# Moving the down projection of a two-layer network's FFN ahead of the up projection of the same step

## The chip, the cores and the metric

The kernel runs on one core of a Trainium2 chip. The metric is device time in microseconds (us) for one execution of the whole program. A core has five engines that run their own instruction streams and wait for each other by semaphores: TensorE (PE, matrix products; its weight loads are listed apart as PEld), VectorE (DVE), ScalarE (ACT), GpSimd (POOL) and SyncE (SP), which here issues the weight transfers.

## The reference

Two blocks of two layers each work on 256 tokens of width 1024. The second block's layers end in a convolutional FFN, which is the part that matters here (D_FF is 3072, the convolution spans 3 tokens):

```python
def conv_ffn(x, norm, w_up, dw_w, dw_b, w_down):
    h = rms_norm_2(x, norm) @ w_up
    g = causal_dwconv(h[..., :D_FF], dw_w, dw_b)
    u = h[..., D_FF:]
    return (jax.nn.gelu(g) * u) @ w_down

def second_block(...):
    for layer in range(DEPTH):
        ...                                   # mixer_ab or conformer_conv
        x = x + cross_attn(...)
        x = x + conv_ffn(...)
    return rms_norm_2(x, final_norm)
```

## The kernel before

**Stages.** The program runs through stages L0, L1 (first block), AB, X0, F0, C, X1, F1 (second block) and the final norm. F0 and F1 are the two FFNs. Each engine has its own function with the same stages written out in order, so the order of the source is the order of each engine's queue.

**Weights.** All weights go through one stream of units of 128 x 1024 numbers, listed in order by `weight_order()`. SP loads unit n into one of 5 raw buffers (`RAW`) once the unit 5 in front has been split. A unit is then split for an exact product: ACT copies it to `weights_hi` (line 485), DVE subtracts that to get `weights_lo` (line 915). There are 4 buffers of split units (`SPLIT`), and ACT may write one only when PE is done with the unit 4 in front. The function `splitter` decides where ACT and DVE stand in their queues with this: before an engine waits for a tile of PE (`for_tile`), it emits the splits of all units which that tile needs and of up to three units behind them. Where one engine waits for a mark of the other (`after_vec`, `after_act`), it emits the splits that the other had emitted by then.

**Products.** Each product is three passes: hi x hi, lo x hi, hi x lo. `proj_F` (line 1467) makes 512 output features x 256 tokens with the weights standing in PE: 4 units of 24 products of 256 columns. `proj_T` (line 1449) makes tokens x 512 features with the activations standing: its products have 512 columns, 12 to a unit.

**The FFN** takes the 3072 inner features in six chunks j of 512. For chunk j there are a gate projection g j, an up projection u j (both `proj_F`, 4 units each) and a down projection d j (`down`, two `proj_T` of 2 units each), which adds into banks 4 to 7 over all chunks. Between them on ACT and DVE:

- after g j: ACT scales four tiles (line 851), DVE adds the other two taps of the convolution (line 1323, 8 instructions), ACT applies the gelu (line 854);
- after u j: DVE multiplies u by the gelu's result (line 1328, two instructions, one for each bank), ACT copies the product to the high part (line 841), DVE makes the low part (line 1331), which is marked `h{j}lo`.

`down(j)` waits for `h{j}lo` ahead of its first product, since both parts are read from the start:

```python
                def down(j):
                    for n in range(2):
                        proj_T("o", 2 * n, src=F_HL[j % 2], us=(0, 1), first=j == 0, last=j == 5, ready=f"h{j}lo")
```

g and u use banks 0 to 3 in turn. Behind d 5 the residual is added (line 999). In stage C, which comes after F0, PE starts with a projection of the memory (4 units, `k`) that needs none of it, then transposes the normed tokens (line 1489). After F1 come only the last norm (line 1390) and the store.

Of the kernel before, what the change touches and what calls it, by code (L numbers as in the profile page):

```python
# [16 lines left out]
W = D // 2  # L17
# [92 lines left out]
def build(nc, A, out, known):  # L110
# [5 lines left out]
    with ctx:  # L116
# [124 lines left out]
        def bank(C, name, i=0):  # L241
            return ps[PLACE[C.stage, name, i]]

        def halves(b):
            return b[:, :].rearrange("p (j s) -> p j s", j=2)
# [5 lines left out]
        def weight_order():  # L251

            got = []

            def kmaj(name, lead):
                ap = A[name]
                for i in lead:
                    ap = ap[i]
                return ap.rearrange("(k p) n -> p k n", p=P)

            def col(name, lead, c, us=(0, 1, 2, 3)):
                ap = kmaj(name, lead)
                got.extend((True, ap[:, 2 * u:2 * u + 2, c:c + W]) for u in us)

            def crossed(name, lead):
                for us in ((0, 1), (2, 3)):
                    for n in range(2):
                        col(name, lead, n * W, us)

            def plain(ap):  # L270
                got.append((False, ap))

            def win(l, *at):
                for c in at:
                    col("w_in", (l,), c)

            def chunk(name, lead, j):
                for n in range(2):
                    col(name, lead, n * W, (2 * j, 2 * j + 1))

            for l in range(DEPTH):
                mem_k, mem_v = (lambda: col("w_mem_kv", (l,), 0)), (lambda: col("w_mem_kv", (l,), W))
                if l:
                    mem_k()
                win(l, SBQ, SBK)
                got.append((True, kmaj("w_in", (l,))[:, :, MLI:MLI + 2 * H]))
                win(l, SBV, SBZ)
                if l:
                    mem_v()
                win(l, MLQ, MLK, MLV)  # L290
                if l == 0:
                    mem_k()
                win(l, MLO, MLZ)
                if l == 0:
                    mem_v()
                win(l, RTQ, RTK, RTV, RTZ, GMU, GMV, GMZ)
                plain(A["gm_ws"][l].rearrange("g p q -> p g q"))
                win(l, XAQ, XAZ)
                for b in range(5):
                    win(l, GATE + b * D, GATE + b * D + W)  # L300
                    chunk("w_up", (l, b), 0)
                crossed("w_out", (l,))

            def heads(name):
                return A[name][0].rearrange("h i j -> i h j")

            col("xa_wk_2", (0,), 0)
            for c in (4, 2, 3):
                col("ab_w_in_2", (0,), c * W)
            col("xa_wk_2", (0,), W)  # L310
            plain(heads("b_group_w_2"))
            plain(heads("a_gate_a_w_2"))
            plain(heads("a_gate_x_w_2"))
            for c in (0, 1):
                col("ab_w_in_2", (0,), c * W)
            col("xa_wv_2", (0,), 0)
            for j in (2, 0, 1):
                chunk("ab_w_out_2", (0,), j)
            col("xa_wv_2", (0,), W)
            for l in range(DEPTH):  # L320
                for c in (0, 1):
                    col("xa_wq_2", (l,), c * W)
                crossed("xa_wo_2", (l,))
                if l == 0:
                    col("xa_wk_2", (1,), 0)
                for j in range(7):
                    if j < 6:
                        col("f_w_up_2", (l,), j * W)
                        col("f_w_up_2", (l,), (6 + j) * W)
                    if j:  # L330
                        chunk("f_w_down_2", (l,), j - 1)
                if l == 0:
                    col("xa_wk_2", (1,), W)
                    for c in (2, 0, 3, 1):
                        col("c_w_pw1_2", (0,), c * W)
                    col("xa_wv_2", (1,), 0)
                    for c in (0, 1):
                        col("c_w_pw2_2", (0,), c * W)
                    col("xa_wv_2", (1,), W)
            return got  # L340

        UNITS = weight_order()
        SPLITS = [n for n, (s, _) in enumerate(UNITS) if s]
        NTH = {n: q for q, n in enumerate(SPLITS)}
# [1049 lines left out]
        def _(pe):  # L1394
# [4 lines left out]
            def begin(name, i=0):  # L1399

                before = BEFORE[PC.stage, name, i]
                if before is not None:
                    stage, *tile = before
                    key = ("free", *tile)
                    if SC.has(key, stage):
                        pe.wait_ge(act_done, SC.at(key, stage))
                    elif VC.has(key, stage):
                        pe.wait_ge(vec_done, VC.at(key, stage))
                    else:
                        assert known is None, before  # L1410
                return bank(PC, name, i)

            def end(ins, name, i=0):
                ins.then_inc(pe_done, PC((name, i)))

            def unit(k, m):

                n = at[0]
                at[0] += 1
                PC.unit = at[0]  # L1420
                assert width(n) == k * m
                shape = "p (k m) -> p k m"
                if n not in NTH:
                    pe.wait_ge(raw_full[n % RAW], 16 * (n // RAW + 1))
                    return raw[:, n % RAW, 0:k * m].rearrange(shape, k=k)
                q = NTH[n]
                PC.split += 1
                pe.wait_ge(lo_done, q + 1)
                return [x[:, q % SPLIT, 0:k * m].rearrange(shape, k=k) for x in (w_hi, w_lo)]

            def used(ins, *names):

                ins.then_inc(pe_done, PC(*names))
                PC.marks["unit", at[0] - 1] = PC.n

            def passes(w, src):
                return (w[0], src[0]), (w[1], src[0]), (w[0], src[1])
# [18 lines left out]
            def proj_F(name, i0=0, src=H_HL, us=ALL, first=True, last=True, ready=None):  # L1456

                bs = [halves(begin(name, i0 + i) if first else bank(PC, name, i0 + i)) for i in range(2)]
                for u in us:
                    w = unit(2, W)  # L1460
                    if ready:
                        pe.wait_ge(vec_done, VC.at(ready % u))
                    for f in range(4):
                        i, j = divmod(f, 2)
                        for kk in range(2):
                            for n, (wp, sp_) in enumerate(passes(w, src)):
                                ins = mm(bs[i][:, j, :], wp[:, kk, f * P:(f + 1) * P], sp_[:, 2 * u + kk, :],  # L1467
                                         start=first and u == us[0] and kk == 0 and n == 0 and j == 0,
                                         stop=last and u == us[-1] and kk == 1 and n == 2, skip_group_check=True)
                        if last and u == us[-1] and f == 1:  # L1470
                            end(ins, name, i0)
                    used(ins, *([(name, i0 + 1)] if last and u == us[-1] else []))
# [313 lines left out]
            def ffn(l):  # L1786
                PC.enter(f"F{l}")
                if l == 0:
                    pe.wait_ge(vec_done, VC.at("n_lo3", "X0"))
                    proj_F("k", 0, src=M_HL["X"])  # L1790
                norm_T()
# [4 lines that stand above are left out]

                for j in range(6):
                    proj_F(f"g{j}", ready=None if j else "h_lo%d")
                    proj_F(f"u{j}")
                    if j:  # L1800
                        down(j - 1)
                down(5)

            cross(0)
            ffn(0)
            PC.enter("C")
            proj_F("k", 2, src=M_HL["X"])
# [16 lines left out]
            for n in range(2):  # L1824
                proj_T("o", 2 * n, ready="c_lo%d")
            cross(1)
            ffn(1)
            assert at[0] == len(UNITS)

# [34 lines left out]
```

## Time and profile before

| | us |
|---|---|
| median of three executions | 1998.99 (1995.81 to 1999.39) |
| the profiled execution, its own time | 1998.05 |
| its span, first to last instruction | 1995.9 |
| PE busy | 1794.4, 90% of the span |
| DVE busy | 1231.1, 62% |
| ACT busy | 1030.6, 52% |

The page divides the span into busy time by engine and then follows back the chain of work that ended last, step by step to what released each. The chain says which engine sets the time in a stretch; the share of busy time says only how much work there is. The clock that the page grants to TensorE is given as a share of full speed: 1.00 is 2.4 GHz, 0.50 is 1.2 GHz.

### The profile page before, as it was taken

To read this page: it belongs to the slowest core of one execution; us is meant where nothing else is said; L and a number is where in the kernel's file an instruction comes from. 1 tells how busy PE (TensorE), PEld (TensorE's weight loads), DVE (VectorE), ACT (ScalarE), POOL (GpSimd) and SP (SyncE) were. 2 spreads that over 40 slices of the span, in tenths; PEclk is the share of its full clock that TensorE was granted. 3 is DMA by queue.
4 is the path that set the end of the run, shared out by engine and by line. 5 is a ranking of instruction groups with operands and counts; after the bars stand their busy time and mean duration, and the time that the engine had idled before them with its cause. 6 is when DMAs were issued, how large, how long until landed. Compare 5 with 4: busy or idle time off the path is not lost.

```text
span 1995.9 us, 26512 instructions
## 1 busy us (share of the span) xinstructions
PE 1794.4 (90%) x10479; PEld 1588.8 (80%) x10479; DVE 1231.1 (62%) x1661; ACT 1030.6 (52%) x1389; POOL 32.6 (2%) x58
## 2 busy tenths in 40 slices
PE   6799999999999999999899699999999307989998
PEld 6688888877888888888689688899999206879997
DVE  3564766656546476565757555566665995546665
ACT  4655555454656555645464655555455104545544
POOL 4000000000000000000000000000000000000000
PEclk9989999999999999999999899999999657989999
DMA  7345545555453454555554353455655102335563
GB/s 255 95 148 169 165 135 185 166 169 198 152 168 127 148 168 136 185 162 177 179 162 140 127 197 112 151 185 168 203 179 180 43 21 93 118 116 183 167 206 110
DMA packets 161915, 306.73 MB, mean 154 GB/s; under 512 B 12323, under 2 KB 16325, under 8 KB 161665
## 3 DMA queue, kind: packets, MB, share of 16 engines
q1 hardware_dynamic: 158928, 298.91, 46.2%
q0 software_dynamic: 2864, 6.14, 0.9%
q8 instruction: 83, 1.36, 0.3%
q14 instruction: 40, 0.32, 0.0%
HBM read 303.97 MB, written 1.05 MB: 153 GB/s over the span
## 4 chain that ended last, share of the span: by engine, by line
PE 75%; DVE 14%; ACT 8%; issue 2%; POOL 0%; DMA 0%; DVEq 0%; ACTq 0%; POOLq 0%
PE bank L1449 42%; PE bank L1467 26%; DVE arena L1360 4%; DVE weights_lo L915 3%; ACT weights_hi L485 1%; PE bank L1760 1%; ACT arena L502 1%; PE bank L1742 1%; DVE h_lo L952 1%; PE bank L1531 1%; ACT spatial_weights L512 0%; PE bank L1489 0%; DVE arena L1179 0%; ACT arena_parts L549 0%; DVE arena_parts L958 0%
## 5 line engine op out<-in xcount | busy, mean ns | idle before, releaser
L915 DVE TENSOR_TENSOR weights_lo<-weights_raw,weights_hi 128x1024 fp32r<-128x1024 f32 x562 | 675.0, 1222 | 550.6 <-ACT weights_hi L485 548.0
L485 ACT ACTIVATE weights_hi<-weights_raw 128x1024 fp32r<-128x1024 f32 x562 | 583.1, 1055 | 499.3 <-PE bank L1449 336.4
L1467 PE MATMUL bank<-h_hi,weights_hi 128*128 128x256 f32 x1504 | 434.0, 289 | 41.2 <-DVE weights_lo L915 21.5
L1467 PE MATMUL bank<-h_hi,weights_lo 128*128 128x256 f32 x1504 | 431.3, 287 | 0.0
L1467 PE MATMUL bank<-h_lo,weights_hi 128*128 128x256 f32 x1504 | 431.2, 287 | 0.0
L1449 PE MATMUL bank<-weights_hi,h_hi 128*128 128x512 f32 x928 | 372.5, 401 | 36.8 <-DVE weights_lo L915 20.1
L1449 PE MATMUL bank<-weights_lo,h_hi 128*128 128x512 f32 x928 | 367.5, 396 | 0.0
L1449 PE MATMUL bank<-weights_hi,h_lo 128*128 128x512 f32 x928 | 366.9, 395 | 0.0
L1467 PEld LDWEIGHTS bank<-h_hi,weights_hi 128*128 128x128 f32 x1504 | 294.7, 196 | 45.3 <-DVE h_lo L952 18.7
L1449 PE MATMUL bank<-weights_hi,arena_parts 128*128 128x512 f32 x928 | 294.8, 394 | 34.0 <-DVE weights_lo L915 34.0
L1467 PEld LDWEIGHTS bank<-h_hi,weights_lo 128*128 128x128 f32 x1504 | 295.1, 196 | 0.4
L1467 PEld LDWEIGHTS bank<-h_lo,weights_hi 128*128 128x128 f32 x1504 | 294.5, 196 | 0.0
L1449 PEld LDWEIGHTS bank<-weights_hi,h_hi 128*128 128x128 f32 x928 | 178.4, 192 | 78.3 <-DVE weights_lo L915 19.6
L1449 PEld LDWEIGHTS bank<-weights_hi,arena_parts 128*128 128x128 f32 x928 | 176.6, 190 | 71.6 <-DVE weights_lo L915 34.8
L1449 PEld LDWEIGHTS bank<-weights_hi,h_lo 128*128 128x128 f32 x928 | 178.0, 192 | 38.3
L1449 PEld LDWEIGHTS bank<-weights_lo,h_hi 128*128 128x128 f32 x928 | 178.5, 192 | 36.2
L1449 PE MATMUL bank<-weights_lo,arena_parts 128*128 128x512 f32 x464 | 182.6, 394 | 0.0
L502 ACT ACTIVATE arena<-bank 128x512 f32<-128x512 f32 x166 | 99.1, 597 | 117.6 <-PE bank L1449 94.0
L1449 PEld LDWEIGHTS bank<-weights_lo,arena_parts 128*128 128x128 f32 x464 | 88.3, 190 | 17.9
L1360 DVE SCALAR_TENSOR_TENSOR arena<-arena,vector_columns 128x255 f32<-128x255 f32 (+14 forms) x240 | 91.5, 457 | 0.0
L1467 PE MATMUL bank<-arena_parts,weights_hi 128*128 128x256 f32 x384 | 70.1, 283 | 0.8 <-DVE x_tokens L999 0.8
L1467 PEld LDWEIGHTS bank<-arena_parts,weights_hi 128*128 128x128 f32 x384 | 60.3, 192 | 1.4 <-DVE x_tokens L999 1.2
(286 smaller groups left out, 1375.8 us busy)
## 6 DMA issues: line engine op xcount, KB each, us to landing
weights_raw<-in_w_in_dram SPq DMA_DIRECT2D x224, 512.0 KB, 3.9
weights_raw<-in_f_w_up_dram SPq DMA_DIRECT2D x96, 512.0 KB, 4.4
weights_raw<-in_f_w_down_dram SPq DMA_DIRECT2D x48, 512.0 KB, 4.1
weights_raw<-in_w_up_dram SPq DMA_DIRECT2D x40, 512.0 KB, 4.2
weights_raw<-in_c_w_pw_dram SPq DMA_DIRECT2D x24, 512.0 KB, 3.8
weights_raw<-in_ab_w_in_dram SPq DMA_DIRECT2D x20, 512.0 KB, 3.7
weights_raw<-in_w_mem_kv_dram SPq DMA_DIRECT2D x16, 512.0 KB, 3.7
weights_raw<-in_w_out_dram SPq DMA_DIRECT2D x16, 512.0 KB, 3.8
```

Source lines behind the costliest of these rows:

```text
L485: nc.scalar.activation(w_hi[:, q % SPLIT, 0:w], raw[:, n % RAW, 0:w], ACT.Copy).then_inc(hi_done, 1)
L502: link(nc.scalar.activation(dst, (view(b) if view else b[:, :]), func, **kw), ("free", name, i), *marks)
L915: tt(w_lo[:, q % SPLIT, 0:w], raw[:, n % RAW, 0:w], w_hi[:, q % SPLIT, 0:w].bitcast(F32), ALU.subtract)\
L952: link(stt(h_lo[:, k, :], b[:, j, :], c[:, col + k:col + k + 1], h_hi[:, k, :].bitcast(F32), ALU.mult, ALU.subtract), *([("free", "hT", i) ...
L1360: stt(y[:, ft, d:S], feat(2, 2)[:, ft, 0:S - d], cols2[:, c:c + 1], y[:, ft, d:S], ALU.mult, ALU.add)\
L1449: ins = mm(bs[t][:, :], sp_[:, 2 * u + kk, t * P:(t + 1) * P], wp[:, kk, :], start=first and u == us[0] and kk == 0 and n == 0, stop=last ...
L1467: ins = mm(bs[i][:, j, :], wp[:, kk, f * P:(f + 1) * P], sp_[:, 2 * u + kk, :], start=first and u == us[0] and kk == 0 and n == 0 and j == ...
L1531: ins = mm(b[0:H, c * S:(c + 1) * S], wp[:, k, c * H:(c + 1) * H], sp_[:, k, :], start=k == 0 and n == 0, stop=k == KD - 1 and n == 2)
L1742: ins = mm(b[:, t, :], q[:, 2 * h + d, t * P:(t + 1) * P], k[:, 2 * h + d, :], start=d == 0, stop=d == 1)
L1760: ins = mm(b[:, d, :], v[:, m, c:c + P], sec(8, 2)[:, h * 512 + m * S:h * 512 + (m + 1) * S], start=m == 0, stop=m == 1)
```

## The change

In both FFNs the down projection of chunk j-1 moves from behind u j to between g j and u j. The weight stream is reordered in the same way.

```diff
@@ weight_order
                 for j in range(7):
                     if j < 6:
                         col("f_w_up_2", (l,), j * W)
-                        col("f_w_up_2", (l,), (6 + j) * W)
                     if j:
                         chunk("f_w_down_2", (l,), j - 1)
+                    if j < 6:
+                        col("f_w_up_2", (l,), (6 + j) * W)
@@ the FFN on PE
                 for j in range(6):
                     proj_F(f"g{j}", ready=None if j else "h_lo%d")
-                    proj_F(f"u{j}")
                     if j:
                         down(j - 1)
+                    proj_F(f"u{j}")
                 down(5)
```

So PE's order g0 u0 g1 u1 d0 g2 u2 d1 ... g5 u5 d4 d5 becomes g0 u0 g1 d0 u1 g2 d1 u2 ... g5 d4 u5 d5. Lines behind the first edit move by one: 1449 becomes 1450, and so on.

**PE at the end of an FFN.** The last chunk of F1 before: g5 ends in bank 1, u5 fills banks 2 and 3, d4 and then d5 add into banks 4 to 7.

```order
L1467 MATMUL bank1<-h_lo,weights_hi 128x256
L1467 MATMUL bank2<-h_hi,weights_hi 128x256 [waits lo_done,vec_done]
...
L1467 MATMUL bank3<-h_lo,weights_hi 128x256
L1449 MATMUL bank4<-weights_hi,arena_parts 128x512 [waits vec_done,lo_done]
...
L1449 MATMUL bank7<-weights_hi,arena_parts 128x512
L1449 MATMUL bank4<-weights_hi,arena_parts 128x512 [waits vec_done,lo_done]
```

And in the changed kernel, at the same place:

```order
L1468 MATMUL bank1<-h_lo,weights_hi 128x256
L1450 MATMUL bank4<-weights_hi,arena_parts 128x512 [waits vec_done,lo_done]
...
L1450 MATMUL bank7<-weights_hi,arena_parts 128x512
L1468 MATMUL bank2<-h_hi,weights_hi 128x256 [waits lo_done,vec_done]
...
L1468 MATMUL bank3<-h_lo,weights_hi 128x256
L1450 MATMUL bank4<-weights_hi,arena_parts 128x512 [waits vec_done,lo_done]
```

Before, the 48 products of d4 stand between the last product of u5 and d5; now d5 is the next thing behind u5, and its first product waits for DVE.

**DVE at the same place.** Before, from the last instruction of g5's convolution (line 1323) to the residual (line 999):

```order
L1323 SCALAR_TENSOR_TENSOR arena<-bank,vector_columns,arena 128x254
L915 TENSOR_TENSOR weights_lo<-weights_raw,weights_hi 128x1024 x4
L1328 TENSOR_TENSOR arena<-bank,arena 128x512 x2
L1331 TENSOR_TENSOR arena_parts<-arena,arena_parts 128x1024
L915 TENSOR_TENSOR weights_lo<-weights_raw,weights_hi 128x1024 x5
L999 TENSOR_TENSOR x_tokens<-bank,x_tokens 128x512 x4
```

And now:

```order
L1324 SCALAR_TENSOR_TENSOR arena<-bank,vector_columns,arena 128x254
L916 TENSOR_TENSOR weights_lo<-weights_raw,weights_hi 128x1024 x8
L1329 TENSOR_TENSOR arena<-bank,arena 128x512 x2
L1332 TENSOR_TENSOR arena_parts<-arena,arena_parts 128x1024
L916 TENSOR_TENSOR weights_lo<-weights_raw,weights_hi 128x1024
L1000 TENSOR_TENSOR x_tokens<-bank,x_tokens 128x512 x4
```

The four splits of one down projection have moved from behind the multiplication with u5 to ahead of it. The same holds on ACT and for chunks 1 to 4.

## Rows read from the trace of the kernel before

**Rows 1.** The page: span, busy time by engine, chain by engine.
```profile
span 1995.9 us, 26512 instructions
PE 1794.4 (90%) x10479; PEld 1588.8 (80%) x10479; DVE 1231.1 (62%) x1661; ACT 1030.6 (52%) x1389; POOL 32.6 (2%) x58
PE 75%; DVE 14%; ACT 8%; issue 2%; POOL 0%; DMA 0%; DVEq 0%; ACTq 0%; POOLq 0%
```

**Rows 2.** Chain that ended last, in order of time: start, us, what.
```profile
497.40 12.68 PE bank L1449 x48
...
1304.39 26.18 PE bank L1467 x216
1330.57 10.91 PE bank L1449 x48
1341.48 23.03 PE bank L1467 x192
...
1466.33 21.79 PE bank L1449 x96
1488.12 11.51 PE bank L1467 x96
...
1966.72 21.80 PE bank L1449 x96
```

**Rows 3.** What PE waited for, 1304.5 to 1488 us: total, times, longest.
```profile
PE bank L1467 <- DVE weights_lo L915: 0.2, 1, 0.2
```

**Rows 4.** DVE in order of time, last chunk of F0.
```profile
1461.13 4.74 DVE L915 TENSOR_TENSOR weights_lo<-weights_raw,weights_hi 128x1024 fp32r<-128x1024 f32 x4 [2.34 <-ACT weights_hi L485]
1465.79 1.41 DVE L1328 TENSOR_TENSOR arena<-bank,arena 128x512 f32<-128x512 f32 x2
1468.39 1.23 DVE L1331 TENSOR_TENSOR arena_parts<-arena,arena_parts 128x1024 fp32r<-128x1024 f32 x1 [1.20 <-ACT arena_parts L841]
```

**Rows 5.** ACT in order of time, last chunk of F0.
```profile
1458.88 1.06 ACT L854 ACTIVATE arena<-arena 128x1024 f32<-128x1024 f32 x1 [2.81 <-DVE arena L1323]
...
1467.23 1.06 ACT L841 ACTIVATE arena_parts<-arena 128x1024 fp32r<-128x1024 f32 x1 [2.62 <-DVE arena L1328]
```

**Rows 6.** DVE in order of time, last chunk of F1.
```profile
1968.78 1.22 DVE L1331 TENSOR_TENSOR arena_parts<-arena,arena_parts 128x1024 fp32r<-128x1024 f32 x1 [1.20 <-ACT arena_parts L841]
```

**Rows 7.** PE in order of time, products that ended a gap (in brackets).
```profile
296.96 0.47 PE L1449 MATMUL bank<-weights_hi,h_hi 128*128 128x512 f32 x1 [1.91 <-DVE weights_lo L915]
...
432.52 0.79 PE L1449 MATMUL bank<-weights_hi,h_hi 128*128 128x512 f32 x1 [3.44 <-DVE weights_lo L915]
...
497.40 0.77 PE L1449 MATMUL bank<-weights_hi,h_hi 128*128 128x512 f32 x1 [4.08 <-DVE h_lo L965]
...
1233.82 2.66 PE L1760 MATMUL bank<-arena 128*128 128x256 f32 x7 [2.05 <-ACT arena L502]
...
1282.27 0.49 PE L1467 MATMUL bank<-h_hi,weights_hi 128*128 128x256 f32 x1 [2.62 <-DVE h_lo L952]
```

**Rows 8.** Busy time by stretch: us, engines, granted clock, DMA share, GB/s.
```profile
296.96:300.40 3.44, 3.44 (x15) 2.89 (x16) 3.26 (x3) 1.54 (x3) 0.00 (x0) 1.00 0.68 213
497.40:500.60 3.20, 3.20 (x8) 2.55 (x9) 1.81 (x2) 0.00 (x0) 0.00 (x0) 0.50 0.58 235
500.70:504.10 3.40, 3.40 (x17) 2.80 (x16) 0.99 (x1) 1.06 (x1) 0.00 (x0) 1.00 0.37 142
1282.30:1285.70 3.40, 3.40 (x16) 3.40 (x17) 2.03 (x5) 2.98 (x5) 0.00 (x0) 0.51 0.02 5
1285.70:1289.10 3.40, 3.40 (x30) 3.40 (x29) 2.07 (x2) 1.06 (x1) 0.00 (x0) 0.99 0.35 89
1304.40:1466.30 161.90, 161.90 (x1177) 154.33 (x1178) 102.93 (x115) 81.06 (x88) 0.00 (x0) 1.00 0.57 187
```

**Rows 9.** DVE in order of time, behind d5 of F0 in stage C.
```profile
1493.90 0.75 DVE L938 TENSOR_SCALAR arena<-x_tokens,statistics 128x1024 f32<-128x1024 f32 x1 [0.56 <-ACT statistics L518]
```

**Rows 10.** DVE in order of time, chunk 4 of F0, behind u4.
```profile
1434.45 1.22 DVE L1331 TENSOR_TENSOR arena_parts<-arena,arena_parts 128x1024 fp32r<-128x1024 f32 x1 [1.20 <-ACT arena_parts L841]
1435.71 2.36 DVE L915 TENSOR_TENSOR weights_lo<-weights_raw,weights_hi 128x1024 fp32r<-128x1024 f32 x2
```

## The prediction

> **What bounds the kernel now.** I read the page first: PE is busy for 90% of the span, and 75% of the chain that ended last is PE's [rows 1]. An average says nothing about the two FFNs, so I then read the chain in order of time. From 1304.39 us to 1488.12 us, which is F0 from the last unit of u0 on, it consists of PE products without a break: g and u pairs of 23.03 us (192 products, so 11.52 us for a projection of 96 and 2.88 us for each of its 4 units), down projections of 10.91 us (48 products, 2.73 us a unit), and at the end d4 and d5 together in 21.79 us [rows 2]. The list of what PE waited for in that stretch has a single entry of 0.2 us, for a split [rows 3]; it stands in u0, where the order doesn't change. The granted clock there is 1.00 for the whole of the stretch up to u5's end [rows 8]. So TensorE is the bound of the FFN, it works at the upper clock of 2.4 GHz, and no wait is left in it that a new order could take away. F1 repeats the pattern, with d4 and d5 in 21.80 us [rows 2]. The question is then only whether the new order opens gaps.
>
> **What the change moves, part by part.** The work is the same: the same 12 units a chunk, the same products, splits and transfers. What changes is the PE work that covers each of two chains on ACT and DVE.
>
> *The chain behind u j, inside the FFN (j = 0 to 4).* In F0, u5 ends at 1466.33, where d4 starts in the chain [rows 2]. Its multiplications end at 1465.79 + 1.41 = 1467.20, the high part runs from 1467.23 for 1.06, the low part from 1468.39 for 1.23 and ends at 1469.62 [rows 4, 5]. The chain is thus 3.3 us behind u's end. Before, d j had g j+1 and u j+1 in front of it (23.03 us); now it has g j+1 alone, 11.52 us. 11.5 covers 3.3 with 8.2 to spare: cost 0. One thing stands in the same queue: DVE goes on with splits only behind the low part. Behind u4 the low part ended at 1434.45 + 1.22, and the next pair of splits began at 1435.71 and took 2.36 [rows 10]. u4 ended 33.94 before u5 (one period: 10.91 + 23.03), at 1432.39, so the first of these splits is there some 4.6 us behind the end of u. PE has three units in stock then, 3 x 2.88 = 8.6 us of g j+1. Cost 0.
>
> *The chain behind g j.* Behind g come the taps, the gelu at 1458.88 for 1.06 [rows 5], and only then the next splits. The first of the four at 1461.13 is done near 1462.3 [rows 4]. g5 ended at 1466.33 - 11.52 = 1454.81; it takes 7.5 us until that split is there. Before, PE lived meanwhile on three units of u5, 8.64 us, so that 1.1 us were left; now it lives on three units of a down projection, 3 x 2.73 = 8.18 us. That leaves 0.7 us. Still enough, so cost 0, but it is the thinnest cover in the new order, and it occurs 10 times (j = 1 to 5, in two FFNs). The gelu itself gains cover: a down projection now stands between g j and u j. It had enough before, so this is worth nothing.
>
> *The chain behind u5.* Here there is no g6. Before, d4 covered it (10.91 us against 3.3). Now d5 is the next thing on PE, and it waits at its first product for the low part. Nothing else is in PE's queue that could go ahead. So PE stands still from u5's end to the end of the low part: 1469.62 - 1466.33 = 3.3 us in F0. F1 has the same chain: 1968.78 + 1.22 = 1970.00 against 1966.72, 3.3 us [rows 2, 6]. Two small things are added. DVE is now held by a split that waits for PE until just before u5's end, as in front of any tile, and the second multiplication can only start when the second bank is there; that is worth some 0.1 us. And a wake-up with the first load of PE costs about 0.1. I take **3.5 us** per FFN. The lower bound is 3.0: the second multiplication (half of 1.41), the copy (1.06) and the low part (1.23) can't start before u5's last bank is complete. The upper bound is 4.7: one split of 1.2 us gets in ahead of the multiplication.
>
> *The clock behind that gap.* This is the second cost. The rows show what gaps of this size do in this kernel. Behind the gap of 4.08 us at 497.40 the granted clock is 0.50 for the next 3.2 us (that is 1.2 GHz) and 1.00 thereafter; behind 2.62 us at 1282.27 it is 0.51 for 3.4 us; behind 1.91 us at 296.96 it stays at 1.00 [rows 7, 8]. All gaps of 2.05 us or more that I found, the ones of 2.05 at 1233.82 and of 3.44 at 432.52 among them [rows 7], were followed by such a low stretch, and none of 1.91 or less. A gap of 3.5 us is well inside. The cost is best read from the projection behind the 4.08 us gap: its 48 products took 12.68 us instead of 10.91 [rows 2], 1.8 us more. That is a down-like projection, the same form as d5. Bounds: 0, if the clock stays; 1.8, if the whole low stretch falls on products. It may begin while PE still stands, then it costs less. I take **1.6 us** per FFN.
>
> On this point the Trainium skill has a rule, in "TensorE: Matmul & The Clock Gate", section "HAM oscillation": idle gaps of PE beyond a few microseconds lower its clock, and the length it names is longer than the gaps of 2.05 and 2.62 us that already did it here. By the page the gap forecast here would be a borderline case, and the sum without the clock term would be 7.0 us; by the rows it is 10.2 us. The measurement decides, and I follow the rows.
>
> *What is late next.* d5 and everything behind it shift by the gap. In F0, PE goes from d5 straight into the `k` projection (11.51 us from 1488.12), and the norm, whose last input was ready at 1493.90 + 0.75 = 1494.65, waits 5.0 us for PE, not the reverse [rows 2, 9]. So stage C starts behind PE, and the shift passes on in full. In F1 only the residual, norm and store follow d5, in a row. SP's queue: the down units come 4 places earlier in the stream, the up units 4 later. The DMA share in F0 is 0.57 [rows 8] and the buffers are refilled at the same pace; cost 0.
>
> **Sum.** 2 x (3.5 + 1.6) = 10.2 us. The profiled execution took 1998.05 us (span 1995.9, 2.15 around it), so it would become 2008.3. Its time is 0.94 below the median of the three runs, 1998.99; against that median I forecast 1998.99 + 10.2 = **2009.2 us**, 0.5% slower. A change of this kernel can be told from no change from about 0.2% on, 4 us.
>
> **The rivals.**
>
> A. The forecast: two gaps, each with a low stretch. With 3.3 to 3.8 for the gap and 0.9 to 1.8 for the clock: 8.4 to 11.2 us, or 2007.4 to 2010.2; with the bounds of both, 3.0 to 4.7 and 0 to 1.8, it is 6.0 to 13.0. Chance 0.76.
>
> B. The gaps come, but the clock stays up behind them (the page's rule read strictly, or the low stretch falls on the idle time): 2 x 3.5 = 7.0, 2006.0 us; with one of two, 2007.6. Against it: all the gaps of 2.05 us or more in these rows. Chance 0.08.
>
> C. The thin cover behind g j breaks: the fourth unit of the down projection is late. That takes over 0.7 us more in the chain of taps, convolution, gelu and split. In u0 there is such a case: there PE waited 0.2 us in spite of longer units [rows 3]. If 0.5 us are missing each time, 10 x 0.5 = 5.0 us come on top: 2014.2 us. Against it: the chain doesn't change, only the units above it get shorter. Chance 0.09.
>
> D. The other side: no slower, within 0.2%. The mechanism would be that the work behind d5 takes up the gap, so that PE's late start doesn't reach the end. It decides only from the point where stage C has over 5.1 us in which PE waits for something that d5 doesn't feed, and F1's tail as well, since one FFN alone would still leave 5.1 us: 1998.99 + 5.1 = 2004.1, slower. Both together give 1999.0. For it speaks that PE waits long in stage C for a convolution on DVE; but that convolution comes behind the projections of C, which come behind d5. Against it are rows 9 and the bare tail of F1. Chance 0.05, most of it for the half case.
>
> E. The new order helps in a way that I don't see, for instance by spreading splits: the only wait it could remove is 0.2 us per FFN [rows 3]. Time 1998.6. Chance 0.02.
>
> **Numbers.** The likeliest case gives 2009.2. To hold 8 in 10, with some 2 us for the scatter of the runs (1995.81 to 1999.39) on either side, the range takes in A and most of B: 2005.0 to 2012.8. Slower by over 0.2% (above 2003.0) are A, B, C and the half case of D (0.03), less 0.02 for the scatter of the runs: 0.94. Within 0.2%: 0.04, the rest of D and that scatter. Faster: 0.02.
>
> **What would show it.** In the changed kernel's trace the PE list should have two new gaps of about 3.5 us, each in front of a product of line 1450 in the last chunk, released by DVE's line 1332, and the granted clock should be 0.50 for about 3.4 us behind them. The down projections d5 should take near 12.6 us instead of 10.9. Chunks 1 to 5 should still be without a break: a wait of PE for weights_lo in a down projection would be C. In stage C the chain should run on as before, some 5 us later. The prediction fails if the clock stays at 1.00, if PE waits inside the loop, or if the span grows by less than the two gaps.

## The result, and the profile after

The changed kernel takes 2007.68 us (median of 5, 2007.22 to 2012.15); the kernel before, timed beside it, 1996.91 us (1994.71 to 1999.39). The ratio is 1.0058, 95% interval 1.0043 to 1.0073: slower by 11.6 us, with 8.6 to 14.6 us as the interval (the two medians differ by 10.8). The profiled execution took 2007.68 us with a span of 2005.5 us, against 1998.05 and 1995.9 before, 9.6 us more.

The page of the kernel after, span and busy time (compare [rows 1]):

```profile
span 2005.5 us, 26512 instructions
PE 1796.5 (90%) x10479; PEld 1590.2 (79%) x10479; DVE 1230.6 (61%) x1661; ACT 1031.6 (51%) x1389; POOL 32.7 (2%) x58
PE 75%; DVE 14%; ACT 8%; issue 2%; DMA 0%; POOL 0%; DVEq 0%; ACTq 0%; POOLq 0%
```

Nothing on this page names the loss: the instruction counts, the shares and the busy times are nearly those of before. It is in the chain in order of time (compare [rows 2]), of which the last chunk of F0 and of F1 read:

```profile
1454.76 10.91 PE bank L1450 x48
1465.67 11.52 PE bank L1468 x96
1479.24 1.24 DVE arena_parts L1332
1480.61 12.74 PE bank L1450 x48
1493.35 11.51 PE bank L1468 x96
...
1970.45 11.52 PE bank L1468 x96
1984.02 1.24 DVE arena_parts L1332
1985.39 12.77 PE bank L1450 x48
```

d4 (10.91) comes ahead of u5 (11.52), and behind u5 the chain leaves PE for the low part on DVE. d5 then takes 12.74 and 12.77 us, where d4 and d5 together took 21.79 [rows 2], 10.9 each. PE in order of time and DVE in order of time show the gap and what fills it:

```profile
1480.61 0.47 PE L1450 MATMUL bank<-weights_hi,arena_parts 128*128 128x512 f32 x1 [3.43 <-DVE arena_parts L1332]
```

```profile
1475.49 1.23 DVE L916 TENSOR_TENSOR weights_lo<-weights_raw,weights_hi 128x1024 fp32r<-128x1024 f32 x1 [1.65 <-ACT weights_hi L486]
1476.63 1.41 DVE L1329 TENSOR_TENSOR arena<-bank,arena 128x512 f32<-128x512 f32 x2
1479.24 1.23 DVE L1332 TENSOR_TENSOR arena_parts<-arena,arena_parts 128x1024 fp32r<-128x1024 f32 x1 [1.19 <-ACT arena_parts L842]
```

u5 ends at 1477.19, where it starts in the chain plus its 11.52. Multiplications, copy and low part end at 1479.24 + 1.23 = 1480.47, with the split of 1475.49 just ahead of them: 3.28 us behind u5, against 3.29 in [rows 4]. The first product of d5 follows 0.14 us later, at 1480.61, and the gap is 3.4 us. The busy time by stretch shows the clock (compare [rows 8]):

```profile
1304.40:1477.19 172.79, 172.78 (x1224) 163.11 (x1224) 107.39 (x119) 85.48 (x92) 0.00 (x0) 1.00 0.59 192
1477.19:1480.61 3.42, 0.00 (x1) 0.03 (x1) 2.05 (x3) 2.50 (x3) 0.00 (x0) 1.00 0.55 158
1480.61:1484.50 3.89, 3.89 (x10) 3.10 (x11) 1.23 (x1) 0.90 (x1) 0.00 (x0) 0.56 0.08 14
1484.50:1493.35 8.85, 8.85 (x41) 7.30 (x41) 4.92 (x6) 4.52 (x7) 0.00 (x0) 1.00 0.40 116
```

F0 from the last units of u0 up to the gap runs at 1.00 (2.4 GHz) without a break, and the clock is still 1.00 in the gap itself. The 3.9 us behind the gap have a mean of 0.56, nearly all of it at 1.2 GHz; then the clock is back. From g0's start to d5's end F0 took 205.85 us before and 211.13 now, 5.28 more; F1 206.99 and 212.16, 5.17 more. Together 10.45 us. The remaining -0.85 us of the 9.6 between the two profiles stands in stages that are the same in both.

### The profile page after: what moved, and what is told of

Read it like the earlier page. It is cut to its first block, busy times and chain, and to the rows that moved or that the text cites. A ratio compares the mean times of both kernels' runs of the same rounds, so it can differ in the third digit from the quotient of the medians.

```text
span 2005.5 us, 26512 instructions
## 1 busy us (share of the span) xinstructions
PE 1796.5 (90%) x10479; PEld 1590.2 (79%) x10479; DVE 1230.6 (61%) x1661; ACT 1031.6 (51%) x1389; POOL 32.7 (2%) x58
## 4 chain that ended last, share of the span: by engine, by line
PE 75%; DVE 14%; ACT 8%; issue 2%; DMA 0%; POOL 0%; DVEq 0%; ACTq 0%; POOLq 0%
PE bank L1450 42%; PE bank L1468 26%; DVE arena L1361 4%; DVE weights_lo L916 3%; ACT weights_hi L486 1%; PE bank L1761 1%; ACT arena L503 1%; PE bank L1743 1%; DVE h_lo L953 1%; PE bank L1532 1%; ACT spatial_weights L513 0%; PE bank L1490 0%; DVE arena L1180 0%; ACT arena_parts L550 0%; DVE arena_parts L959 0%
```

## The experiments

Times are given against the kernel before, run beside each.

**The last chunk as before.** Chunks 1 to 4 have the new order, the last chunk the old one; `weight_order` has the same condition.

```diff
                 for j in range(6):
+                    late = j == 5
                     proj_F(f"g{j}", ready=None if j else "h_lo%d")
-                    if j:
+                    if j and not late:
                         down(j - 1)
                     proj_F(f"u{j}")
+                    if j and late:
+                        down(j - 1)
                 down(5)
```

> Chunks 1 to 4 keep the new order (g, down, u), the last chunk has the old one (g5 u5 d4 d5). Theory (all the loss stands behind u5, the inner chunks are covered): PE runs through both FFNs without a gap but for the 0.2 us in u0, the clock stays at 1.00, and the time equals the kernel before: 0 us, ratio 1.000, within 2 us. Rival (the new order costs something in every chunk, by late splits or the weight stream): a good part of the 10 us remains, at least 3 us, with PE waiting for weights_lo in the down projections.

1996.88 us against 1996.87, ratio 1.0002 (0.9994 to 1.0011). Its chain runs through the end of F0 without leaving PE:

```profile
1397.00 23.03 PE bank L1471 x192
1420.03 10.91 PE bank L1453 x48
1430.94 34.55 PE bank L1471 x288
1465.49 21.79 PE bank L1453 x96
```

F0 takes 205.85 us, to the hundredth what it took before. Four of the five swapped steps cost nothing, and gain nothing.

**The last chunk alone.** The reverse condition, `late = j < 5`.

> The reverse: chunks 1 to 4 in the old order, only the last chunk in the new one (g5 d4 u5 d5). Theory: the whole loss comes from here, +10 us against before (8.5 to 11.5), with two gaps of 3.4 us and d5 at 12.7 us, as in the changed kernel. Rival (cost in every chunk): clearly less than 10 us.

2007.5 us, ratio 1.0061 (1.0048 to 1.0074), the same as the full change. The chain has the same gap and the same slow d5:

```profile
1465.11 11.52 PE bank L1471 x96
1478.67 1.24 DVE arena_parts L1335
1480.05 12.74 PE bank L1453 x48
```

The two runs together place the loss: all of it belongs to the last of the five swapped steps.

**One unit held back.** The new order, but in the last chunk one of the four units of d4 stays behind u5.

```diff
                     proj_F(f"g{j}", ready=None if j else "h_lo%d")
-                    if j:
+                    if j and j != 5:
                         down(j - 1)
+                    if j == 5:
+                        proj_T("o", 0, src=F_HL[0], us=(0, 1), first=False, last=False, ready="h4lo")
+                        proj_T("o", 2, src=F_HL[0], us=(0,), first=False, last=False)
                     proj_F(f"u{j}")
+                    if j == 5:
+                        proj_T("o", 2, src=F_HL[0], us=(1,), first=False, last=False)
                 down(5)
```

> The new order, but in the last chunk one of d4's four units (12 products, 2.73 us) stays behind u5. Theory (the gap is what the chain of 3.4 us leaves uncovered, and the clock falls behind a gap of 3.4 us but not behind one below 1.9 us): gap 3.43 - 2.73 = 0.7 us, clock stays at 1.00, d5 10.9 us; +1.4 us for both FFNs. Rival (the low stretch comes with any gap at this place): 2 x (0.7 + 1.8) = +5.0 us.

In the profile the gap was 0.7 us in each FFN, as expected, and the clock stayed at 1.00. But d5 took 11.15 us and not 10.91, and the time was 2001.06 us, ratio 1.0026 (1.0015 to 1.0037): 3.0 to 7.4 us more, where the two gaps and 0.24 us in each d5 make 1.9. By its time alone this is the rival of the expectation (+5.0 us, a low stretch behind any gap at this place); the profile contradicts it, since the clock stayed at 1.00 in d5. The same kernel was run once more.

> The kernel with one unit of d4 behind u5 once more. Its F0 and F1 took only some 1 us each more than before, but its time was 5.2 us (3.0 to 7.4) longer, and the profiled execution was 4 us late already at the start of F0, in code that is the same. If that was chance (the low stretches of the clock falling otherwise in the unchanged stages), the ratio comes out near 1.001 now; if it belongs to this kernel, it comes out near 1.0026 again.

1999.78 us, ratio 1.0024 (1.0014 to 1.0035). The loss belongs to this kernel; it wasn't the chance of one session. The busy time of d5 in this run, with its clock, and the chain around it:

```profile
1477.89:1489.02 11.13, 11.13 (x50) 9.25 (x51) 7.29 (x8) 6.38 (x9) 0.00 (x0) 1.00 0.45 144
```

```profile
1462.94 11.53 PE bank L1473 x96
1476.52 1.24 DVE arena_parts L1337
1477.89 11.13 PE bank L1455 x48
```

The gap of 0.7 us and the 0.22 us in d5 are all that F0 lost here, and the profiled span is 1.7 us longer than that of before. The two ratios say 5.2 and 4.8 us; without the 1.9 us in the FFNs about 3 us are left (some 1 to 5 by the intervals) for which the FFNs have no place. That part stays open; what is known of it is in the last section.

**Products in the gap.** The new order, with PE kept busy while it waits.

```diff
+                pe.wait_ge(vec_done, VC.at(("free", "g5", 0)))
+                b = bank(PC, "g5", 0)
+                for _ in range(24):
+                    mm(b[:, 0:S], h_hi[:, 0, 0:P], h_hi[:, 0, :], start=True, stop=True)
                 down(5)
```

> The new order, with 24 extra products of 256 columns (2.88 us at full clock) between u5 and d5, into a free bank, their result unused. They do no useful work; d5 still starts when its input is there. Theory (gap and clock are two separate terms): d5 starts as late as in the changed kernel, 3.4 us behind u5, but the clock stays at 1.00 and d5 takes 10.9 us: 2 x 3.4 = +6.9 us against before, 3.7 less than the changed kernel. Rival (d5's 12.7 us come from something else, such as its first weights or banks): d5 stays at 12.7 us, +10.5 us.

2004.29 us, ratio 1.0045 (1.0031 to 1.0059): 9.0 us slower than the kernel before (6.2 to 11.8), where 6.9 were expected, and 3.2 us below the last chunk alone by the medians of the same session. The two FFNs of its profile took 7.4 us more than before. PE in order of time, and the stretch of d5:

```profile
1478.27 3.04 PE L1806 MATMUL bank<-h_hi 128*128 128x256 f32 x24
1481.87 0.47 PE L1450 MATMUL bank<-weights_hi,arena_parts 128*128 128x512 f32 x1 [0.56 <-DVE arena_parts L1332]
```

```profile
1481.87:1493.01 11.14, 11.14 (x50) 9.24 (x51) 6.15 (x7) 5.42 (x8) 0.00 (x0) 1.00 0.35 95
```

d5 starts 3.42 us behind u5 (1466.92 + 11.53 = 1478.45), as late as in the changed kernel, but it takes 11.14 us instead of 12.74. This takes the terms apart: 3.4 us of gap, 1.6 us of clock (12.74 - 11.14), and some 0.24 us (11.14 - 10.91) that d5 takes longer behind a wait at full clock too. The last term I had not counted as such. It is called the restart below.

**The last chunk by halves.** The gap attacked from the other end: the chain itself gets shorter.

```diff
 # ACT, for the last chunk
+                        for i in range(2):
+                            at = slice(2 * i, 2 * i + 2)
+                            act.wait_ge(vec_done, after_vec(f"h5m{i}"))
+                            link(nc.scalar.activation(F_HL[1][0][:, at, :], feat(1)[:, at, :], ACT.Copy), f"h5hi{i}")
 # DVE, likewise the subtraction; PE
-ready=f"h{j}lo")
+ready=f"h{j}lo" if j < 5 else "h5lo%d")
```

> The new order, but behind u5 the high and the low part are made in two halves, and each unit of d5 waits only for the half that it reads. Theory (d5 is held by the chain multiply, multiply, copy, subtract; halving it lets the first unit go): chain to the first half about 0.3 (first multiplication ends) + 0.7 (second) + 0.7 (half a subtraction) = 1.7 us behind u5 instead of 3.4, below the gaps that cost the clock, so +3.4 us against before for both FFNs. If the clock falls all the same: +7 us. Rival (fixed costs of the added instructions eat the gain): gap near 3 us, +9 us.

2001.77 us, ratio 1.0027 (1.0016 to 1.0037). The waits of PE, ACT's halves, and the stretch of d5:

```profile
PE bank L1462 <- DVE arena_parts L1341: 1.7, 1, 1.7
```

```profile
1480.90 0.63 ACT L845 ACTIVATE arena_parts<-arena 128x512 fp32r<-128x512 f32 x1 [1.89 <-DVE arena L1335]
1481.68 0.63 ACT L845 ACTIVATE arena_parts<-arena 128x512 fp32r<-128x512 f32 x1 [0.16 <-DVE arena L1335]
```

```profile
1482.47:1493.62 11.15, 11.15 (x50) 9.25 (x51) 6.79 (x8) 6.72 (x9) 0.00 (x0) 1.00 0.40 127
```

The gap is halved to 1.7 us, as expected, the clock stays, and F0 took 207.85 us from g0 to the end of d5, 2.0 more than before. With F1 that is about 4 us, inside the interval of 3.2 to 7.4.

**The cover behind g, in both orders.** Two copies on ACT whose result is not used stand ahead of each gelu, once in the new order and once in the old.

```diff
+                    for _ in range(2):
+                        link(nc.scalar.activation(junk, junk, ACT.Copy))
                     link(nc.scalar.activation(sec(j % 2), sec(j % 2), ACT.Gelu_apprx_tanh), f"gelu{j}")
```

> The new order, with two extra copies of 128x512 on ACT (about 0.6 us each, result unused) ahead of every gelu: 1.2 us more in the chain behind g. Theory (cover behind g is three units of the projection that follows, here a down projection of 2.73 us a unit, with 0.7 us to spare): PE waits 1.2 - 0.7 = 0.5 to 0.6 us in the fourth unit of every d 0 to d 4, 10 times, and 1.2 us more in u0, twice: +8 us on top of the changed kernel, +18 us against before. Rival (the spare time is the same in both orders): the same addition as in the old order with the same copies.

> The kernel before with the same two extra copies ahead of every gelu. Theory (cover is three units of u, 2.88 us each, with 1.1 us to spare): PE waits 0.1 to 0.2 us in the fourth unit of u1 to u5, 10 times, and 1.2 us more in u0, twice: +4 us against before, so some 4 us less than the copies cost in the new order. Rival (same spare time in both orders): both grow by the same amount.

New order: 2020.48 us, ratio 1.0119 (1.0105 to 1.0133). Old order: 2006.36 us, ratio 1.0050 (1.0036 to 1.0063). What PE waited for in F0, first in the new order, then in the old (total, times, longest):

```profile
PE bank L1452 <- DVE weights_lo L918: 3.7, 5, 0.8
PE bank L1452 <- DVE arena_parts L1334: 3.4, 1, 3.4
PE bank L1470 <- DVE weights_lo L918: 1.6, 1, 1.6
```

```profile
PE bank L1469 <- DVE weights_lo L917: 3.0, 6, 1.6
```

In u0 both wait 1.57 us where they waited 0.24 (PE in order of time has two decimals), so the copies put 1.33 us into the chain. In chunks 1 to 5 the new order waits 3.7 / 5 = 0.74 us each time, the old one (3.0 - 1.6) / 5 = 0.28. The difference, 0.46 us, is that of the covers: 3 x (2.88 - 2.73) = 0.45. What each order had to spare follows: 1.33 - 0.28 = 1.1 us in the old, 1.33 - 0.74 = 0.6 us in the new. The theory of the cover held; the sizes of my expectation (+18 and +4 us against 23.8 and 10.0 measured) were too low, for two reasons that the rows show: the copies cost 1.33 and not 1.2, and each wait costs PE more than its own length. The chain of either kernel, the unit behind a wait:

```profile
1327.27 1.24 DVE weights_lo L918
1328.55 3.02 PE bank L1452 x12
```

```profile
1328.52 1.24 DVE weights_lo L917
1329.80 3.14 PE bank L1469 x24
```

3.02 instead of 2.73 and 3.14 instead of 2.88, 0.26 to 0.29 us more for the first unit, at full clock. It is the term found with the products in the gap. In the old order it closes the sum of F0: 1.33 in u0, five waits of 0.28 and five restarts of 0.26 make 4.03 us, and F0 took 209.88 us, 4.03 more than before.

**A version that beats both.** If a held-back unit covers a gap, it can do so where the kernel before has gaps of its own. In five stages (AB, X0, F0, C, X1) PE waits behind the transposes of the normed tokens [rows 7 has the one at 1282.27]. The edit is shown for stage C; the other four are changed alike, and the FFNs are those of before.

```diff
-            proj_F("k", 2, src=M_HL["X"])
+            proj_F("k", 2, src=M_HL["X"], us=(0, 1, 2), last=False)
             norm_T()
+            proj_F("k", 2, src=M_HL["X"], us=(3,), first=False)
```

> The kernel before, FFN untouched. In the five stages where PE makes a projection of the memory ahead of the transposes of the normed tokens (AB, X0, F0, C, X1) the last of its four units now stands behind the transposes, where PE waited for the low part of the norm. Theory (a held-back unit covers a gap, and a gap below 2 us doesn't lower the clock): the gaps 3.75, 1.62, 2.62, 1.61 and 1.61 us shrink to 1.0, 0, 0, 0 and 0, about 10 us, and the two low stretches behind the first and the third go, 1.6 us each: -10 to -14 us against before, ratio 0.993 to 0.995. Rival (the transposes then wait for the norm, since they come 2.7 to 2.9 us earlier): the gap only moves ahead of the transposes, less than 5 us gained.

1986.24 us against 1995.80, ratio 0.9958 (0.9945 to 0.9970): 8.4 us faster, 6 to 11. That is less than expected (10 to 14 us, ratio 0.993 to 0.995). The waits of PE over the whole span that changed, and the start of F0 with its clock:

```profile
PE bank L1489 <- DVE arena L938: 8.5, 2, 5.7
...
PE bank L1467 <- DVE h_lo L952: 5.8, 2, 3.8
```

```profile
1277.76:1290.70 12.94, 12.94 (x110) 12.94 (x110) 8.92 (x13) 9.48 (x14) 0.00 (x0) 1.00 0.51 160
```

The waits for the norm's low part (line 952) fell from 17.0 to 5.8 us in total; those of the transposes (line 1489) rose from 5.7 to 8.5. That is the rival's effect, in one stage of five: in AB the transposes now come too early and wait 2.8 us themselves, where the gap was to shrink from 3.75 to 1.0, and the clock is low behind that wait as it was behind the old one:

```profile
1037.76:1041.16 3.40, 3.40 (x17) 3.40 (x18) 2.84 (x3) 3.24 (x6) 0.00 (x0) 0.53 0.58 192
```

So 1.8 us of gap and the 1.6 us of one low stretch, both counted on in the expectation, did not come. In the other four stages the gap is gone. At F0 the low stretch that followed the gap of 2.62 us [rows 7, 8] is gone with it, the clock is 1.00.

## Why the prediction was right

The time was forecast at 2009.2 us in a range of 2005.0 to 2012.8 and measured at 2007.68; the difference at 10.2 us, measured 11.6 (8.6 to 14.6) by the ratio and 10.45 in the two FFNs of the profile. The time came out below the forecast and the difference above it because the kernel before, the base of the sum, had a median of 1998.99 in three executions and of 1996.91 in five. By its steps:

- **No wait in the FFN that a new order could take away.** Right: with the last chunk as before, F0 takes 205.85 us in both orders.
- **The chain behind u j and behind g j is covered in chunks 0 to 4.** Right. That the cover behind g is the thinnest, with 0.7 us left against 1.1, was measured: 0.6 and 1.1 us. Rival C had a real mechanism: more than 0.6 us of added work on ACT opens a wait at ten places.
- **The gap behind u5: 3.5 us.** It was 3.4 in both FFNs. Of the two small additions of 0.1 us, the wake-up is there, 0.14 us from the end of the low part to the first product. The delay of the multiplications is not: with the split just ahead, they ended as far behind u5 as before.
- **The clock: 1.6 us.** That a low stretch comes and costs 1.6 us (12.74 - 11.14) was argued before and is shown now, by the run with products in the gap, where gap and start stayed and only the clock changed. The number is partly luck. The row behind it (12.68 against 10.91, 1.8 us) holds a restart too, which was not known then; what was taken off the 1.8 was for a low stretch that begins while PE stands, and that did not happen: the clock in the gap is 1.00. d5 as a whole was forecast near 12.6 and took 12.74 and 12.77, at the upper bound of 1.8 us above 10.91 or just over it.
- **"All gaps of 2.05 us or more" lower the clock.** This reading of the rows was too strong. In the same trace PE stands for 5.37 us ahead of its product at 20.06 us, and the clock is 1.00 in that gap and behind it. In the ten other profiles the gap of 2.05 us that stands at 1233.82 in [rows 7] was followed by no low stretch. For gaps of 3.4 us in the FFN the reading held all six times that a profile has one.
- **Everything behind d5 shifts in full.** Right in F0: the `k` projection starts right behind d5, at 1493.35. Of the shift of 5.2 us the profile still shows 4.5 at the start of F1's g0 (1786.00 against 1781.53), since low stretches at the end of stage C fell otherwise.
- **Rival B** (clock stays) needs a shorter gap: it is what happened at 0.7 and 1.7 us. **Rival D** (absorbed behind) didn't occur.

The sum came out close because two errors offset in part: the gap was 0.1 too long, the restart of 0.24 was missing. What remains unexplained is not in this sum but in the version with one unit held back, above.

## What to carry to other kernels

A step that is moved ahead in a software pipeline is free only while something else stands where it stood; look at the last turn of the loop, where the next chunk's work is missing. A gap on TensorE costs its length, a restart, and, if it is long enough (the last section has the counts), a low stretch of the clock behind it, here 3.4 + 0.24 + 1.6 us. So leaving one small piece of independent work behind the last producer can be worth more than its own length: a unit of 2.73 us took 4.3 us off F0 (211.13 to 206.79), though the whole kernel gained less, 11.6 us of loss becoming about 5. Before reordering, compare for each wait the work of the engine that covers it with the chain that it covers: when both orders cover it, as in all but the last chunk here, the order doesn't matter.

## What the runs showed that I had not expected

**A restart costs a quarter of a microsecond.** Behind the waits looked at, of 0.28 to 1.75 us, the next unit of PE took 0.24 to 0.29 us longer at a granted clock of 1.00: d5 11.13 to 11.18 instead of 10.91 behind gaps of 0.6 to 1.7 us, single units 3.02 instead of 2.73 and 3.14 instead of 2.88. The list of waits does not contain it; ten short waits of 0.28 us cost about twice what they seem to. The first products show where it stands. In an unbroken stream the first product of a down projection begins 0.16 us before the last one of the projection ahead has ended (before: d4 at 1466.17, u5 ends at 1466.33), and then one begins each 0.23 us. Behind a wait (one unit held back, second run) nothing is left to overlap with, and the second product comes 0.31 us behind the first:

```profile
1477.89 0.47 PE L1455 MATMUL bank<-weights_hi,arena_parts 128*128 128x512 f32 x1 [0.69 <-DVE arena_parts L1337]
1478.20 0.39 PE L1455 MATMUL bank<-weights_lo,arena_parts 128*128 128x512 f32 x1
```

0.16 + 0.08 make the 0.24 us. The ends of products are modelled in the profile, so the border between gap and restart is uncertain; their sum, here 0.94 us in F0, is not.

**The same code in the stages ahead takes up to 5 us more or less.** F0's g0 started at 1281.43 us in one profiled execution and at 1286.27 in another, after 1280 us of the same instructions. The low stretches fall otherwise: the stretch of the kernel with one unit behind, and the same stretch of the kernel before, are

```profile
297.00:301.00 4.00, 3.75 (x10) 3.00 (x11) 3.51 (x4) 1.41 (x2) 0.00 (x0) 0.57 0.70 205
```

```profile
297.00:301.00 4.00, 4.00 (x18) 3.33 (x19) 3.22 (x3) 2.10 (x3) 0.00 (x0) 1.00 0.76 235
```

So a gap of about 1.9 us [rows 7] costs the clock in some executions and not in others. The same holds for one of 2.05 us, here behind the gap of [rows 7] in the kernel before and behind the same gap with the last chunk as before:

```profile
1233.82:1237.22 3.40, 3.40 (x10) 2.78 (x11) 0.35 (x1) 0.79 (x2) 0.00 (x0) 0.61 0.02 5
```

```profile
1234.65:1238.05 3.40, 3.40 (x16) 3.02 (x17) 0.94 (x2) 1.17 (x2) 0.00 (x0) 1.00 0.02 5
```

Over the eleven profiles, and for gaps that begin at a clock of 1.00: those of 1.5 to 1.75 us were never followed by a low stretch, those of 1.91 us in 5 of 22 cases, those of 2.05 us in 8 of 22, those of 2.6 to 4.1 us always. There is no sharp border between them. The gap of some 5.4 us ahead of the product at 20.06 us, behind which seven of the profiles show no low stretch, is an exception that no run explains. These patterns are probably much of the scatter of the runs.

**The open 3 us of the version with one unit held back.** Its second profile is only 1.7 us longer than that of the kernel before, but that profile is itself a late one: 1998.05 us, where the medians of the kernel before in these two sessions are 1996.87 and 1995.80. Against a profile of a fast execution, that of the last chunk as before (1994.60 us, the same time in F0), it is 5.1 us longer, and only 1.9 of them stand in the FFNs. Most of the rest, 2.5 us, lies between the end of F0 and the start of F1, where the code is that of before: 293.3 us in both profiles of this version, 290.8 with the last chunk as before, 290.4 to 293.4 in the other profiles without an edit there, with 293.4 in the kernel before. The mean granted clock of its executions was lower too, 0.9474 (7 executions) and 0.9485 (8) against 0.9494 (17) and 0.9497 (12) of the kernel before beside them. Both fit low stretches that fall unfavourably in stages C and X1 more often than in the kernel before. Why a shift of 0.9 us should do that is not shown, and the cause stays open.
